# The front of a three-layer block on one core: mixer and memory projections as one stream of weight tiles

## What is computed

```python
mod = silu(c) @ w_ada + b_ada                    # [2048] @ [2048, 6*2048]
sh1, sc1, gt1, sh2, sc2, gt2 = split(mod, 6)
h = rmsnorm(x, g_mix) * (1 + sc1) + sh1
x = x + gt1 * hybrid_mixer(h, ...)               # pool, attention (8 heads), LRU; then @ w_out
h = rmsnorm(x, g_ffn) * (1 + sc2) + sh2
x = x + gt2 * ((silu(conv(h @ w_gate)) * (h @ w_up)) @ w_down)
x = rmsnorm(x, final_g)
for l in range(2):
    mk, mv = split(mem @ w_mem_kv[l])            # mk normed by head; used by branch M of layer l
    x = x + layer(x, mk, mv, ...)                # four gated branches, w_out
```

## Time and profile before

| what | us |
|---|---|
| median of 3 runs | 3338.24 |
| the profiled execution | 3341.34 |
| its span, first to last instruction | 3339.4 |
| first matmul of a tile | 33.42 |
| first matmul of the feed-forward part | 752.93 |
| PE busy over the span | 3117.6 |
| DVE busy | 1996.6 |
| ACT busy | 1471.2 |

### The profile page before, as it was taken

One profiled execution on the slowest core, in us unless ns is written; L12 is line 12 of the kernel. 1 busy time (PEld: TensorE's weight loads), 2 busy tenths in 40 slices (PEclk: granted clock), 3 DMA queues, 4 the chain that ended last, 5 costly groups with the idle time before them and its releaser, 6 DMA issues.

```text
span 3339.4 us, 39152 instructions
## 1 busy us (share of the span) xinstructions
PE 3117.6 (93%) x14234; PEld 2581.7 (77%) x14234; DVE 1996.6 (60%) x1972; ACT 1471.2 (44%) x1701; POOL 56.3 (2%) x110
## 2 busy tenths in 40 slices
PE   5677698669999999999999999999999999999999
PEld 4566575558888888888888888888888888888887
DVE  6757832764565656576655556556557555565564
ACT  2232233334444544455544444454445445444543
POOL 1101100000000000000000000000000000000000
PEclk9778897889999999999999999999999999999999
DMA  9849950554555555555555554555555555545555
GB/s 369 344 176 364 371 192 0 223 187 164 193 189 189 183 188 189 189 185 168 177 183 177 192 189 152 193 170 190 188 163 178 182 177 190 189 151 193 172 183 189
DMA packets 164824, 654.61 MB, mean 196 GB/s; under 512 B 18416, under 2 KB 18576, under 8 KB 151648
## 3 DMA queue, kind: packets, MB, share of 16 engines
q1 hardware_dynamic: 149840, 547.03, 48.8%
q0 software_dynamic: 14864, 105.88, 8.0%
HBM read 650.74 MB, written 2.10 MB: 195 GB/s over the span
## 4 chain that ended last, share of the span: by engine, by line
PE 85%; DVE 6%; DMA 5%; issue 2%; ACT 2%; SPq 0%; DVEq 0%; POOLq 0%; ACTq 0%
PE pg L879 25%; PE pg L881 25%; PE pg L880 25%; DMA R<-w_ada 4%; DVE R L1462 3%; DMA w_raw<-w 1%; PE pm L925 1%; PE pm L984 1%; PE pm L969 1%; PE pm L1294 1%; DVE w_lo L1343 1%; DVE R L1615 0%; PE pm L947 0%; PE pm L951 0%; PE pm L1188 0%
## 5 line engine op out<-in xcount | busy, mean ns | idle before, releaser
L1343 DVE TENSOR_TENSOR w_lo<-w_raw,w_hi 128x1024 fp32r<-128x1024 f32 x1028 | 1256.5, 1225 | 1100.0 <-ACT w_hi L447 1095.1
L447 ACT ACTIVATE w_hi<-w_raw 128x1024 fp32r<-128x1024 f32 x1028 | 1089.5, 1060 | 1694.3 <-PE pg L881 1515.1
L879 PE MATMUL pg<-w_hi,hT_hi 128*128 128x512 f32 x3232 | 1274.0, 394 | 49.6 <-DVE w_lo L1343 41.0
L881 PE MATMUL pg<-w_hi,hT_lo 128*128 128x512 f32 x3232 | 1262.8, 391 | 0.0
L880 PE MATMUL pg<-w_lo,hT_hi 128*128 128x512 f32 x3232 | 1262.7, 391 | 0.0
L879 PEld LDWEIGHTS pg<-w_hi,hT_hi 128*128 128x128 f32 x3232 | 610.5, 189 | 182.0 <-issue 39.6
L881 PEld LDWEIGHTS pg<-w_hi,hT_lo 128*128 128x128 f32 x3232 | 609.5, 189 | 128.3
L880 PEld LDWEIGHTS pg<-w_lo,hT_hi 128*128 128x128 f32 x3232 | 610.3, 189 | 123.7
L879 PE MATMUL pg<-w_hi,y_parts 128*128 128x512 f32 x864 | 337.5, 391 | 1.4 <-issue 1.4
L881 PE MATMUL pg<-w_hi,y_parts 128*128 128x512 f32 x864 | 336.4, 389 | 0.0
L880 PE MATMUL pg<-w_lo,y_parts 128*128 128x512 f32 x864 | 336.1, 389 | 0.0
(11 more groups left out here) (268 smaller groups left out, 1334.4 us busy)
## 6 DMA issues: line engine op xcount, KB each, us to landing
w_raw<-w SPq DMA_DIRECT2D x1028, 512.0 KB, 3.5
R<-w_ada POOLq DMA_DIRECT2D x96, 1024.0 KB, 10.7
R<-mem_T SPq DMA_DIRECT2D x1, 2048.0 KB, 20.2
x_rows<-x SPq DMA_DIRECT2D x1, 2048.0 KB, 26.6
out<-x_rows SPq DMA_DIRECT2D x4, 512.0 KB, 5.2
con_sb<-con SPq DMA_DIRECT2D x1, 1472.0 KB, 7.4
small_w_sb<-small_w POOLq DMA_DIRECT2D x2, 576.0 KB, 4.9
R<-con POOLq DMA_DIRECT2D x1, 1024.0 KB, 5.1
```

The costliest lines, as they stand in the source:

```text
L447: act.activation(w_hi[:, g % RING, :, :].rearrange("p c n -> p (c n)"), raw[:, g % RING, :], ACT.Copy).then_inc(hi_done, 1)
L879: pe.matmul(out, hi, w_hi[:, slot, c, :], start=start, stop=False)
L881: return pe.matmul(out, lo, w_hi[:, slot, c, :], start=False, stop=stop)
L1343: tt(flat(w_lo[:, g % RING, :, :]), raw[:, g % RING, :], flat(w_hi[:, g % RING, :, :]).bitcast(F32), ALU.subtract).then_inc(lo_done, 1)
```

## The change

- **One stream.** The 136 front tiles run in the order mk0, mv0, x, y, p, q0, k0, v0, q1, k1, v1, the four groups of `w_out`, mk1, mv1 (`FRONT`, `F_TILES`). On every engine a function `upto(t)` issues tiles until number t, and each small step stands at a tile number of its own. The loops over groups and the sections of the front are gone. The first two groups of `w_out` are interleaved (six tiles each, then two each).
- **Modulation.** `w_ada` is laid out anew in chunks of 128 x 1024 (512 KB), a ring of five, twelve half-sixths in the order of `HALVES`, with the bias of the two gates as a chunk of its own: 196 chunks. Half 0 is weighed beside tiles 0 to 15, halves 1 to 3 (48 chunks) in one run after tile 19, halves 4 to 9 one chunk a tile beside tiles 22 to 117, halves 10 and 11 beside the first feed-forward groups. The sums are in two buffers. The gates are spread by ones times `ada_acc`, with no diagonal and no column sum.
- **Norm 1** runs beside the first memory groups, and its modulation is applied to `hf_1` in SBUF (`modulated`). ACT instead of DVE rounds to `hT_hi`, in pieces (`refill`), and DVE makes `hT_lo` (`lower`, `lower_4`), so that a group can start on the first piece.
- **Memory of layer 1** runs as the last two groups, beside the second norm; `mem_T` (2 MB) is loaded a second time at tile 104. The second norm's transposes stand at tiles 127 to 130.
- Loads at the start: `vec`, `mem_T` in four pieces, four tiles, then 256 of the constants' columns and `x`; the rest of the constants at tile 30.

```diff
+FRONT = ("mk0", "mv0", "x", "y", "p", "q0", "k0", "v0", "q1", "k1", "v1", "o0", "o1", "o2", "o3", "mk1", "mv1")
+HALVES = ((1, 0), (0, 0), (1, 1), (0, 1), (4, 0), (3, 0), (2, 0), (2, 1), (4, 1), (3, 1), (5, 0), (5, 1))
+CHUNKS = [(h, k) for h, (q, _) in enumerate(HALVES) for k in range(-1 if q in (2, 5) else 0, KD)]
...
         @block.sync
-            sp.dma_start(con[:, :], t["con"]).then_inc(consts_in, 16)
             sp.dma_start(vec[:, :], t["vec"]) ...
+            for p in range(4):
+                sp.dma_start(mem_f[:, 4 * p:4 * p + 4, :], t["mem_T"][:, 4 * p:4 * p + 4, :]).then_inc(mem_in[p], 16)
...
+                if g == 104:
+                    sp.wait_ge(y_ready, 2)
+                    sp.dma_start(mem_f1, t["mem_T"]).then_inc(mem1_in, 16)
...
         @block.gpsimd
+            for i, (h, k) in enumerate(CHUNKS):
+                if i >= ADA_RING:
+                    pool.wait_ge(ada_used, i - ADA_RING + 1)
+                pool.dma_start(ada_ring[:, i % ADA_RING, :], t["w_ada"][i]).then_inc(ada_in[i % ADA_RING], 16)
...
         @block.scalar
+            def upto(t):
+                nonlocal fed
+                while fed < t:
+                    g = fed
+                    act.wait_ge(raw_in[g % RING], 16 * (g // RING + 1))
+                    if g >= RING:
+                        act.wait_ge(tile_used, g - RING + 1)
+                    act.activation(w_hi[...], raw[:, g % RING, :], ACT.Copy).then_inc(hi_done, 1)
+                    ...
+                    refill_at(g)
+                    fed += 1
...
+            for q in range(GT):
+                upto(131 + q // 2)
+                rows_T(1, q, hf_2, True)
+            upto(FT + RING)
+            head_std(1, 8)
...
         @block.tensor
+            upto(20)
+            pe.wait_ge(mod_taken, 2)
+            ada_sums(2, 0)
+            ada_sums(3, 1)
+            upto(24)
...
+            attn_at(61, 0, Zv[0], 6, 0)
+            upto(71)
+            broadcast(6, 2)
...
-            pe.wait_ge(section, END_NORM2)
-            group(G_FF, 0, hT)
+            pe.wait_ge(evac_act, F_ACTS[FRONT.index("mk1")])
+            group(G_FF, 0, hT, P_FF)
...
         @block.vector
+            upto(20)
+            for k in range(KD):
+                weigh(1, k)
+                if k == 3:
+                    take_mod(0, 0)
+            take_mod(1, 1)
+            scale_gain(16, V("g_mix")[:, 0:8], 2)
+            dve.wait_ge(hf_done, GT)
+            modulated(0)
+            modulated(1)
+            for k in range(2):
+                weigh(2, k)
+            lower_4(P_MIX, hf_1)
+            lower_4(P_MIX + 1, hf_1)
+            for k in range(2, KD):
+                weigh(2, k)
+            for k in range(KD):
+                weigh(3, k)
+                ...
+                if k in (4, 9):
+                    upto(21 + k // 9)
+            take_mod(3, 1)
+            scale_gain(24, V("g_mix")[:, 8:16], 4)
+            modulated(2)
+            modulated(3)
+            lower_4(P_MIX + 2, hf_1)
+            lower_4(P_MIX + 3, hf_1)
...
+            upto(124)
+            dve.wait_ge(ssq_done, FRONT_SSQ)
...
+            upto(FT)
+            mem_heads(1)
+            upto(FT + RING)
             step(dve.memset(flat(F_acc), 0.0))
```

More of the change, by code:

```diff
@@ L122 @@
 _at = 0
-for _name, _n in (("causal", TB * S), ("tri", TB * S), ("row", 8 * P)):
+for _name, _n in (("causal", TB * S), ("tri", TB * S)):
     CON1[_name] = (_at, _at + _n)
@@ L389, in tiles @@
                                  ).then_inc(raw_in[g % RING], 16)
-            tiles(0, True)
-            with sp.Fori(1, GROUPS) as group:
+            with sp.Fori(G_FF, GROUPS) as group:
                 tiles(group)
@@ new lines, in rows_T @@
+            def rows_T(occ, q, dest, scaled):
+                act.wait_ge(rowsT_ps, occ * GT + q + 1)
+                for c in range(KC):
+                    k = q * KC + c
+                    src = pm[q % 4][:, c * S:(c + 1) * S]
+                    if scaled:
+                        i = act.activation(dest[:, k, :], src, ACT.Identity, bias=mod[:, 48 + k:49 + k],
+                                           scale=mod[:, 64 + k:65 + k])
+                    else:
+                        i = act.activation(dest[:, k, :], src, ACT.Copy)
+                i.then_inc(hf_done, 1)
@@ L617, in _ @@
-            squares(1, xn)
-            transposed(1, hf, gain=mod[:, 64:80], bias=mod[:, 48:64])
-            broadcast(1)
+            act.activation(flat(GR), flat(GR), ACT.Tanh, scale=0.7978845608028654).then_inc(lru_act, 1)
+            upto(51)
+            for q in range(2):
+                act.wait_ge(pool_ps, q + 1)
+                act.activation(flat(pool_d[:, 2 * q:2 * q + 2, :]), pm[2 + q][:, :],
+                               ACT.Copy).then_inc(pool_sb, 1)
+            upto(55)
@@ L903, in short @@
                     last.then_inc(tile_used, 1)
-            def columns(base, n, lhs, free, done, after=None):
-                pe.sem_inc(waited, 1)
-                with pe.Fori(0, n // 2) as j:
-                    for i in range(2):
-                        pe.wait_ge(free, done + j * 2 + i - 1)
-                        group(base + j * 2 + i, i, lhs)
-                    if after is not None:
-                        after(j)
-                if n % 2:
-                    pe.wait_ge(free, done + n - 2)
-                    group(base + n - 1, 0, lhs)
             hT = (hT_hi, hT_lo)
@@ L1512, in _ @@
+            for p in range(4):
+                lower_4(P_MEM0 + p, mem_f)
+                upto(p + 1)
+            upto(9)
+            row_norm(0, TB)
+            for tb in range(TB):
+                i = ts(xn_1[:, tb, :], x[:, tb, :], rstd[:, tb:tb + 1], None, ALU.mult)
+                if tb == 0:
+                    step(i)
+                    step.settle()
+                else:
+                    i.then_inc(rows_ready, 1)
             dve.wait_ge(lam_out, 3)
@@ L1692, in _ @@
                 down_out(g0 + 2, j, 3)
-                step.leave(NFF - 2, 11)
+                step.leave(NFF - 3, 11)
             j = NFF - 2
```

1007 lines of the change are left out of this document (591 added, 416 removed).

## The result

The changed kernel takes **3178.68 us** (median of 4 executions, 3174.02 to 3186.65), the kernel before beside it 3337.03 us (3330.71 to 3343.34). The ratio is **0.9518**, 95% interval [0.9499, 0.9536]. The forecast was 3163 us, 3120 to 3225, faster. The profiled execution has a span of 3175.3 us, at a mean granted clock of 0.981.

What follows compares the result with a forecast made beforehand. Behind 752 us only PE's own work counts, so time lies in the front: 161 + 317 + 70 + 2 + 25 = 575 us. With 2586.5 plus 3 behind it, span 3164.5, forecast 3163 us, range 3120 to 3225.

Steps and rivals of the forecast that it cites:

- Memory of layer 0: First 16 tiles: PE, loads and DVE all end near 70 to 75 us; w_lo of tile 19 at 78.
- Modulation alone: Run of 48 chunks after tile 19: DVE bounds it at 1.27 us a chunk; 83 us, tile 20 at 161.
- Tiles 20 to 135 and small work: 116 tiles 317 us, small matmuls at full clock 70, clock's return at tile 20 2, stalls 25.
- (a): Residual of the first w_out group: PE wants its bank before DVE has done w_lo, a chunk and residual; 1 us.
- (b): Second load of mem_T, 5 us of transfer in the tiles' queue: 1 us of stall.
- (c): Norm 2 at tile 124: DVE waits for squares and root and scales x, with no w_lo meanwhile; 3 us.
- (d): Beside tiles 131 to 134: ACT's rounding, copies and refill take 4.1 us a tile against PE's 2.73; 5 us.
- (e): Seam before tile 136: DVE waits for a square root ACT gives only behind tile 139's rounding; ring drains, 6.5 us.
- (f): Unseen waits in some forty small steps of the front: 8 us.
- Nothing else bounds this stretch: Tiles 20 to 135: DVE (2.28 of PE's 2.73 us a tile) and loads (384 of 418 GB/s) stay below their limits.
- Costly small steps: Rival, chance 0.2: small matmuls between tiles lower the clock and make PE wait; +80 us, 3245.
- Late chunks: Rival, chance 0.07: load latency bounds the run of 48 chunks; +24 us there and some of the start, 3190.

Runs made afterwards that it cites:

- Run 1: Changed kernel with the start's loads as before (constants and x ahead of the tiles; mem_T stays in pieces): 3186.66 us, ratio 0.9533.
- run 12: Changed kernel with mk1's norm at tile 134, tiles between heads' logits, halves 2 and 3 alternating, 1.5 MB of small loads behind tile 12: 3154.76 us, ratio 0.9444.
- run 3: Changed kernel with three slots for the w_ada chunks instead of five: 3208.52 us, ratio 0.9591.
- run 9: Changed kernel with the chunks of halves 2 and 3 alternating, so that products seldom depend on the one before: 3182.49 us, ratio 0.9511.
- run 5: Changed kernel with the norm of mk1 moved from behind the last front tile to tile 134, ahead of the seam: 3165.23 us, ratio 0.9487.
- run 2: Changed kernel with each attention round in one piece, at tiles 68 and 92, without tiles between its steps: 3182.36 us, ratio 0.9524.
- run 10: Changed kernel with only the first chunk of halves 4 to 9 loaded and weighed, 90 of 96 chunks left out: 3175.36 us, ratio 0.9503.
- run 8: Changed kernel without the logits' eight-row matmul for the gate's row, 16 of 32 logit matmuls left out: 3158.51 us, ratio 0.9454.
- run 7: Changed kernel with a tile between one head's logits and the next's, and one between the halves of the f columns: 3171.23 us, ratio 0.9491.

## Why the prediction was right, and what its steps missed

It was right on the sign, the size and, in the main, the mechanism, and 16 us too low. 11 of them are in the span; the rest is that the profiled execution of before lay 3.1 above its median, and this one 1.6 below. Of its signs, PE was busy for over 95% from 165 to 560 us (386.9 of 395) and the gap at the seam came; but the clock there was 0.95 and not 1.00, and 14 of the 32 logit matmuls stood 1.15 us apart, which it had named as a sign of being wrong. What is not shown: no run puts a whole stage of the front back, so how the 169 us divide is read from positions in two executions, and the runs test single terms of it.

- *Start.* 19 us forecast, 20.16 measured. Run 1 shows that an early start reaches tile 20: of 8.3 us, 7.7 do.
- *Memory of layer 0.* The `w_lo` of tile 19 was to be done at 78 and was done at 85.0. **This is the step that failed most, by 7 us**: it put 1.5 MB of small loads behind tile 5 in the tiles' queue at their mean price, not at the moment at which they come. ACT waits 7.5 us there for a tile, DVE 5.9 for its `w_hi`, PE 3.70 at 43.13, and DVE then runs late for the row norm (`L1543`, in run 12 `L1546`):

```profile
40.67 1.06 ACT L564 ACTIVATE w_hi<-w_raw 128x1024 fp32r<-128x1024 f32 x1 [7.52 <-DMA w_raw<-w]
...
41.76 1.22 DVE L1675 TENSOR_TENSOR w_lo<-w_raw,w_hi 128x1024 fp32r<-128x1024 f32 x1 [5.90 <-ACT w_hi L564]
...
49.39 0.17 DVE L1543 TENSOR_SCALAR sc<-sc 128x2 f32<-128x2 f32 x1 [0.32 <-ACT R L496]
```

```profile
43.49 0.17 DVE L1546 TENSOR_SCALAR sc<-sc 128x2 f32<-128x2 f32 x1 [0.30 <-ACT R L498]
```

  Run 12, which moves them behind tile 12, reaches the row norm 5.9 us sooner and ends this stage as much sooner. A slip stands beside it: the prediction's terms for DVE add up to 63 us, and behind a start of some 18 they end at 81 (76 if hT_lo is made before), not near 70 to 75.
- *Modulation alone.* 83 us forecast, 86.1 measured. The bound named was right, but only just: run 3 shows that five slots are enough and three not, and run 9 that the loads stand right behind DVE. The term mis-sized is the period of a dependent product: 1.27 assumed, 1.39 measured, which is 5 us over 45 of them, of which the three plain products (0.75) give 1.6 back. (The terms as written add up to 81.4 and not 83, and waits for loads, 3.1 us, were not among them.)
- *Tiles 20 to 135 and small work.* 317 + 70 + 2 + 25 = 414 forecast, 407.1 + 5.45 = 412.6 measured. That they agree so closely is luck, for the parts were off both ways. The small matmuls' steps cover 74 us, near the 70 forecast; 43 tile matmuls ran at half clock, 8.6 us of loss that my "2 for the clock" did not hold; and the visible stalls were 9 us, not 25. (a) residual: 1.67 against 1. (b) second load of `mem_T`: none seen. (c) norm 2: 1.95 against 3. (d) ACT beside tiles 131 to 134: no pause of PE there, against 5. (e) the seam: 5.45 against 6.5, cause shown by run 5. (f) of the eight us of unseen waits the trace shows none (in attention, run 2 shows why: the helpers work head by head).
- *Nothing else bounds this stretch.* Right: run 10 takes a third of DVE's work and of the bytes away and gains 1.3 us of it by position, and run 8 takes PE's work away and gains all of that. (The 290 us of DVE's work beside tiles 22 to 117 are 267 by their own terms, which only adds to the slack.)
- *Feed-forward part.* +5.1 against +3. Of it 4.6 are small matmuls, 176.9 us instead of 172.2: the eight that spread gate 2 (3.6) and eight transposes of mk1 (1.0), as it named them, somewhat larger than it put them.
- *Rivals.* Costly small steps: the half that is clock came in small (13 us in 210 to 470: 260 us at 0.95), the half that is waiting did not come. Late chunks: not at five slots, but at three. The Trainium skill's rule in "DMA: Bandwidth & Descriptors", section Bandwidth, to batch to 1 MiB, would have spoken against the smaller chunk. Here 512 KB loads landed after 5.6 us, five in flight, and the run of chunks moved 312 GB/s with DVE waiting for loads for 3.1 of its 86 us; a run with chunks of 1 MB is not among these.

What the fall of the clock inside a piece of logits hangs on was shown in part. In the profiled executions with the logits in one piece, the changed kernel's and nine others', the mean clock from 210 to 470 us was 0.93 to 0.97 in eight and 0.99 and 1.00 in two (runs 2 and 5). In the three in which the piece was divided or halved it was 1.00, 1.00 and 0.99. The kernel of before shows the same fall in the same piece, there behind pauses of 0.93 and 0.84 us. So this piece whole puts the clock at risk, and divided or halved it did not lose it in three executions of three. Whether its length or its eight-row matmuls do it is not told apart, the f columns fell divided too, and the whole-span clocks of the executions without a profile overlap (0.981 to 0.986 in run 7, up to 0.983 with the piece whole). What decides in a single execution stays open.

## What to carry to other kernels

Where one engine bounds most of a program and another stage leaves it idle, one stream of tiles with small steps between them pays by what it puts under the tiles, here 96 chunks of DVE work and the mixer's waits, and, in the one place where it was tried (attention), much less by how finely the steps are cut: price the small work, and look for pauses only at what the helpers finish last. Count a load in the tiles' queue at the moment at which it stands there, and a chain of dependent instructions at its start-to-start time. When PE is 100% busy and the granted clock is still below 1.00, look at what kind of matmuls stand there, and try a tile between them: it helped for the logits and not for the f columns.
